# Reordering four stretches of a two-block fp32 transformer kernel: normalization boundaries, memory attention, the first output product, and the scan product

## The chip, the cores and the metric

The kernel runs on one NeuronCore of a Trainium2 chip, in one launch. The metric is the device time of one execution, in microseconds (us). Three runs of the kernel before are shown; their median is what a prediction is compared with. Engines are named as in the profile: PE is TensorE's matmuls, PEld its weight loads, DVE is VectorE, ACT is ScalarE, POOL is GpSimd, SP is SyncE, which here only issues DMAs.

## The reference, cut to what matters

One sequence of 512 positions with 1024 features passes through two blocks. All is fp32.

```
first block:   p = rms_norm(x) @ w_in ; pooling, stick-breaking attention, memory attention, each gated
               kv = rms_norm(mem) @ w_mem_kv     (mem has 256 positions; its q and k are normed per head)
               x = x + concat(pool, stick, memory) @ w_out
second block, for layer 0 and 1:
               m = mixer(rms_norm(x))            (0: retention + neighbourhood attention, 1: SSD scan)
               x = x + rms_norm(m)
               f = conv_geglu(rms_norm(x) @ w_up) @ w_down
               x = x + rms_norm(f)
scan mixer:    xbc = silu(conv5(h @ w_xbc)) ; dt = softplus(h @ w_dt + bias) ; z = h @ w_z ; scans ; @ w_out
rms_norm(v) = v * rsqrt(mean(v^2) + 1e-6) * gain
```

## The kernel before, in words

**Layout.** Activations lie features first: x is 8 tiles of 128 features by 512 positions. Every product runs over weight tiles of 128 output features, and a tile is 8 blocks of 128x128 (22 for the down products).

**Three matmuls for one.** Weights and activations are split into a rounded high part and the rest: ACT copies `w_hi` from the loaded `raw` slot (L309), DVE subtracts to get `w_lo` (L316), over `raw` itself. Each block product is three matmuls (L352 to L354): high by high, high weight by low activation, low weight by high activation. So a tile of 8 blocks is 24 matmuls of 512 columns.

**The ring.** Weights come through a ring of 5 slots. SP loads slot q once PE has finished slot q-5 (L301). `hi_to(act, q)` and `lo_to(dve, q)` emit the splits up to slot q at that point of ACT's or DVE's program; `split_ahead(name, t)` (L326) says how far ahead of tile t they run. Every engine works through its own list in order, and waits on semaphores counted by the others.

**A normed product.** The gain is folded into the activation split, and the norm's factor is applied to the product's rows afterwards. So a product can start before the sum of squares is known. `lead_pe` (L356) works on the first 4 tiles (2 for in1) at once, one block of the contraction at a time, as each low part `a_lo[k]` becomes ready. Later, at tile `SUMS[name][0]` (5 for all), `pre_sums_pe` (L429) sums the squares over partitions with a matmul by ones, into the bank of tile `SUMS[name][1]`; ACT takes Ln and Exp (`roots_act`, L437), and DVE refines the root (`roots_dve`, L443: one halving, three dependent operations). Only then can DVE take or scale the first product tile.

**A boundary** (three of them, `boundary_act` L503 and `boundary_dve` L513): after a mixer or FFN product, the root of its sum of squares comes first, then for each of the 8 tiles k DVE scales `m[k]` (L499), adds it to x (L501), and makes `a_lo[k-1]` (L417); ACT makes `a_hi[k]` (L413) and the square (L421) between. PE meanwhile repeats some matmuls whose result is not used (L486), then waits for the first `a_lo`. At the very end the last root is followed by eight pairs of scale and add, each followed by a store of 256 KB from SP (L2306 to L2308).

**Memory attention and out1** (`one_pe` from L1298, `one_act` from L1446, `one_dve` from L1600): PE interleaves the products of mem_kv, the scores (L1233), the turns of the probabilities (L1247) and the values (L1258) of four steps with the first output product's lead (`out1_half`, 4 tiles together). DVE has in one list the head norms (`half_norm`, `norm`: three dependent operations and one more, L456 to L458 and L1539), the low parts of the mixed activation (L1544), the maxima (`top`, L1550), the reciprocals (`invert`, L1559) and the copies of turned probabilities (`turned`, L1566); ACT has the exponentials (L1399) and the scaling of the probabilities by the reciprocals (`norms`, L1409).

**The first output product's tail** (L2351 to L2355 on ACT, L2398 to L2407 on DVE): for each tile t the lists hold: split slot t+4; add tile t to x; a_hi, square; a_lo and the sum of squares of the tile before. Slots 8 to 11 from the start of out1 are the first four of in2, whose lead comes next.

**The scan product xbc** (24 tiles, `xbc_act` L1804, `xbc_dve` L1832). Beside its lead runs the small product for dt (`dt_part`, 3 matmuls for each k). For each tile DVE scales the PSUM bank (L528), ACT writes the middle tap (L1817), DVE adds four taps (L1840), which frees the bank, and ACT applies silu (L1807). PE needs a free bank for tile 7 on: tile 7 takes the bank of tile 0. After tile 23 come two z tiles, and then `begin(0)` of the scans (L1875), which waits for the silu of all 24 tiles.

```
def split_ahead(name, t):   # name in SUMS, so for xbc too
    return PLAN[name]["slot0"] + max(min(t, 5) + 8, t + AHEAD)
...
for t in range(24):         # xbc_dve
    lo_to(dve, split_ahead("xbc", t))
    scale_dve(dve, "xbc", t, nrm_x[1])
    ...
    if t:
        taps(t - 1)
```

## Time and profile before

| | |
|---|---|
| median of 3 runs | 1825.57 us (1823.8 to 1826.84) |
| the profiled execution | 1822.33 us, of which its span is 1820.6 us |
| PE busy | 1752.2 us (96%), 8246 matmul instructions |
| DVE busy | 1164.6 us (64%) |
| ACT busy | 783.4 us (43%) |
| POOL busy | 177.5 us (10%) |
| memory traffic | 144.44 MB read, 2.10 MB written |
| chain that ended last | PE 80%, DVE 12%, ACT 5% |

PE is busy nearly all the time, so time can come only from the 68 us in which it is not (1820.6 - 1752.2) or in which its granted clock is low (a matmul at the lower clock counts as busy for longer). The idle time is read by stage, since each has another releaser.

### The profile page before, as it was taken

The page shows a single profiled execution, that of the slowest core. Times are in us where ns is not written, and L with a number is a line of the kernel's source. Part 1 is how long each engine was busy: PE and PEld are TensorE (multiplying, and loading weights), DVE is VectorE, ACT ScalarE, POOL GpSimd, SP SyncE. Part 2 cuts the span into 40 slices and gives each one's busy share as a digit, 9 for nine tenths or more (in the row PEclk, how much of TensorE's full clock was granted, in tenths as well). Part 3 has the DMA queues.
Part 4 walks back from the last instruction along what each step waited for, and adds up shares of the span by engine and source line. Part 5 has one row for each costly group of instructions (what it writes and reads, how often), then busy time and mean ns, then how long its engine had stood idle before and what let it go on. Part 6 is the DMA issues. An engine that isn't in the chain of part 4 may idle for free.

```text
span 1820.6 us, 20806 instructions
## 1 busy us (share of the span) xinstructions
PE 1752.2 (96%) x8246; PEld 1371.7 (75%) x8246; DVE 1164.6 (64%) x1577; ACT 783.4 (43%) x1326; POOL 177.5 (10%) x202
## 2 busy tenths in 40 slices
PE   9999898899999999999999999999899999999996
PEld 6777777676667888888877786777578788888884
DVE  4575754776758787663355998576674678766333
ACT  4465642452235454442232453655462445444220
POOL 0311000320000011110000000211220001111000
PEclk9999999999999999999999999999999999999998
DMA  5211223222112332333322222101112132323331
GB/s 215 93 58 47 70 82 108 87 63 66 56 46 73 117 103 93 96 98 101 96 67 87 81 93 69 35 29 43 35 35 93 58 116 94 103 93 93 100 99 55
DMA packets 42752, 147.88 MB, mean 81 GB/s; under 512 B 5152, under 2 KB 6304, under 8 KB 42528
## 3 DMA queue, kind: packets, MB, share of 16 engines
q1 hardware_dynamic: 39168, 138.43, 23.5%
q10 hardware_dynamic: 3488, 8.12, 1.3%
q8 instruction: 66, 1.08, 0.2%
q14 instruction: 30, 0.25, 0.0%
HBM read 144.44 MB, written 2.10 MB: 80 GB/s over the span
## 4 chain that ended last, share of the span: by engine, by line
PE 80%; DVE 12%; ACT 5%; issue 1%; DMA 1%; ACTq 0%; POOL 0%; DVEq 0%
PE bank L352 22%; PE bank L353 22%; PE bank L354 22%; DVE cv L1840 4%; DVE w_lo L316 2%; PE bank L1941 1%; ACT w_hi L309 1%; PE bank L1902 1%; PE bank L1914 1%; PE bank L698 1%; PE bank L711 1%; DVE bank L528 1%; PE bank L1923 1%; PE bank L1187 1%; PE bank L1186 1%
## 5 line engine op out<-in xcount | busy, mean ns | idle before, releaser
L352 PE MATMUL bank<-a_hi,w_hi 128*128 128x512 f32 x1504 | 606.6, 403 | 18.6 <-DVE cv L1840 6.7
L316 DVE TENSOR_TENSOR w_lo<-raw,w_hi 128x1024 fp32r<-128x1024 f32 (+1 forms) x264 | 335.1, 1273 | 413.6 <-ACT w_hi L309 412.8
L354 PE MATMUL bank<-a_hi,w_lo 128*128 128x512 f32 x1504 | 589.8, 392 | 0.0
L353 PE MATMUL bank<-a_lo,w_hi 128*128 128x512 f32 x1504 | 589.7, 392 | 0.0
L309 ACT ACTIVATE w_hi<-raw 128x1024 fp32r<-128x1024 f32 (+1 forms) x264 | 274.1, 1042 | 372.4 <-DMA raw<-in_w_down 142.6
L352 PEld LDWEIGHTS bank<-a_hi,w_hi 128*128 128x128 f32 x1504 | 284.9, 189 | 101.8 <-issue 28.0
L353 PEld LDWEIGHTS bank<-a_lo,w_hi 128*128 128x128 f32 x1504 | 284.9, 189 | 64.5 <-issue 7.2
L354 PEld LDWEIGHTS bank<-a_hi,w_lo 128*128 128x128 f32 x1504 | 284.6, 189 | 60.5
L1060 ACT ACTIVATE u<-bank,par 128x512 f32<-128x512 f32 x88 | 68.5, 779 | 176.2 <-DVE bank L528 176.2
L352 PE MATMUL bank<-g_hi,w_hi 128*128 128x512 f32 x352 | 137.0, 389 | 0.0
L353 PE MATMUL bank<-g_lo,w_hi 128*128 128x512 f32 x352 | 137.0, 389 | 0.0
L354 PE MATMUL bank<-g_hi,w_lo 128*128 128x512 f32 x352 | 137.0, 389 | 0.0
L1103 POOL TENSOR_TENSOR gv<-u 128x512 f32<-128x512 f32 x44 | 57.1, 1299 | 564.1 <-DVE u L1079 564.1
L2056 ACT ACTIVATE em<-bank,lbias 128x128 f32<-128x128 f32 x256 | 70.4, 386 | 23.4 <-PE bank L1924 23.1
L2196 DVE TENSOR_TENSOR em<-em,gmat 128x512 f32<-128x512 f32 x64 | 50.0, 787 | 41.6 <-ACT em L2056 41.3
L354 PEld LDWEIGHTS bank<-g_hi,w_lo 128*128 128x128 f32 x352 | 66.1, 188 | 13.8
L353 PEld LDWEIGHTS bank<-g_lo,w_hi 128*128 128x128 f32 x352 | 66.1, 188 | 13.6
L352 PEld LDWEIGHTS bank<-g_hi,w_hi 128*128 128x128 f32 x352 | 66.1, 188 | 13.6
L1840 DVE SCALAR_TENSOR_TENSOR cv<-bank,par,cv 128x510 f32<-128x510 f32 (+1 forms) x96 | 71.7, 748 | 2.5
L1079 DVE SCALAR_TENSOR_TENSOR u<-bank,par,u 128x511 f32<-128x511 f32 x88 | 66.0, 750 | 3.1
L1076 DVE SCALAR_TENSOR_TENSOR u<-bank,par,u 128x511 f32<-128x511 f32 x88 | 65.1, 740 | 0.0
L528 DVE TENSOR_TENSOR bank<-bank,nrm_u 128x512 f32<-128x512 f32 x88 | 60.9, 692 | 0.7 <-PE bank L354 0.7
(362 smaller groups left out, 2096.1 us busy)
## 6 DMA issues: line engine op xcount, KB each, us to landing
raw<-in_w_up SPq DMA_DIRECT2D x88, 512.0 KB, 3.7
raw<-in_w_in SPq DMA_DIRECT2D x52, 512.0 KB, 3.7
raw<-in_w_out SPq DMA_DIRECT2D x32, 512.0 KB, 3.7
raw<-in_w_down SPq DMA_DIRECT2D x32, 512.0 KB, 3.5
raw<-in_w_xbc SPq DMA_DIRECT2D x24, 512.0 KB, 3.7
raw<-in_w_z SPq DMA_DIRECT2D x16, 512.0 KB, 3.6
raw<-in_w_down SPq DMA_DIRECT2D x16, 384.0 KB, 3.1
x<-in_xT ACTq DMA_DIRECT2D x4, 512.0 KB, 7.1
```

The source lines that it names most:

```text
L309: nc.scalar.activation(w_hi[:, q % RING, 0:w], raw[:, q % RING, 0:w], ACT.Copy).then_inc(hi_done, 1)
L316: nc.vector.tensor_tensor(w_lo[:, q % RING, 0:w], raw[:, q % RING, 0:w], w_hi[:, q % RING, 0:w].bitcast(F32), ALU.subtract).then_inc(lo_do ...
L352: nc.tensor.matmul(out, wh, rhs_hi[:, k, :], start=k == first, stop=False)
L353: nc.tensor.matmul(out, wh, rhs_lo[:, k, :], start=False, stop=False)
L354: return nc.tensor.matmul(out, wl, rhs_hi[:, k, :], start=False, stop=stop)
L528: nc.vector.tensor_tensor(tile_bank(name, t)[:, :], tile_bank(name, t)[:, :], r, ALU.mult).then_inc(scaled, 1)
L1060: nc.scalar.activation(u[:, t % 4, :], tile_bank(name, t)[:, :], ACT.Identity, scale=pcol(f"ffn_w{layer}", 3 * t + 1), bias=pcol(f"ffn_b{l ...
L1076: nc.vector.scalar_tensor_tensor(out=ut[:, 1:S], in0=pt_[:, 0:S - 1], scalar=pcol(w, 3 * t), in1=ut[:, 1:S], op0=ALU.mult, op1=ALU.add).th ...
L1079: nc.vector.scalar_tensor_tensor(out=ut[:, 0:S - 1], in0=pt_[:, 1:S], scalar=pcol(w, 3 * t + 2), in1=ut[:, 0:S - 1], op0=ALU.mult, op1=ALU ...
L1103: nc.gpsimd.tensor_tensor(gv[:, i % 2, :], u[:, 2 * i % 4, :], u[:, 2 * i % 4 + 1, :], ALU.mult).then_inc(prod, 1)
L1840: nc.vector.scalar_tensor_tensor(out=dst, in0=tile_bank("xbc", tile)[:, a + by:b + by], scalar=pcol("conv_w", 5 * tile + tap), in1=dst, op ...
L2056: e = nc.scalar.activation(em[:, n % 4, c * P:(c + 1) * P], bank[4 + n % 2][:, c * P:(c + 1) * P], ACT.Exp, bias=lbias[:, c, d, h:h + 1])
```

## The change

Four edits, joined:

1. **Boundaries and closing.** In the three boundaries the low part of tile k-1 stands between the scaling and the addition of tile k, where it stood behind both. At the end DVE scales all eight tiles but adds only three of them; for tiles 0 to 4 PE adds x and the scaled product in PSUM with ten matmuls by the identity (the five by x are issued before the root is known), ACT copies the banks to x, and SP stores those first.
2. **Memory attention's order.** On ACT and DVE the roots and norms of the keys' halves, the reciprocals, the maxima and the turned copies stand in another order, with low parts later; the split of out1's slot 4 stands inside the attention.
3. **First output product's tail.** The one loop is written out: four additions first, then splits and low parts in groups, slots up to 11 at fixed places.
4. **Scan product.** The sum of squares is taken at the last step of the lead (k=7, after the dt matmuls) where it stood before tile 5; ACT's and DVE's splits of slots 5 and 6 stand behind the roots. `split_ahead` for xbc is 5 slots ahead of tiles 0 to 6 (it was 8), then 11, then t+4. DVE scales a tile ahead of the split. The dt transposes stand before tile 5 (6 before).

No matmul, load or element operation is dropped but the five additions of the closing.

```diff
 LEAD = {"in1": 2, "out1": 4, "in2": 4, "out2": 4, "up0": 4, "xbc": 4, "up1": 4}
-SUMS = {"in1": (5, 7), "in2": (5, 7), "up0": (5, 7), "xbc": (5, 6), "up1": (5, 7)}
+SUMS = {"in1": (5, 7), "in2": (5, 7), "up0": (5, 7), "xbc": (4, 6), "up1": (5, 7)}
 DT_BANK, CUM_BANK, TOTAL_BANK, CST_BANK = 0, 3, 4, 5
...
             return PLAN[name]["slot0"] + (8 + t // 2 if t < 8 else t + AHEAD)
+        if name == "xbc":
+            return PLAN[name]["slot0"] + max(min(t, 6) + 5, t + AHEAD)
         return PLAN[name]["slot0"] + max(min(t, 5) + 8, t + AHEAD) if name in SUMS else last_slot(name, t) + AHEAD
...
         for t in range(LEAD[name], PLAN[name]["tiles"]):
-            if t == before:
+            if t == before and name != "xbc":
                 pre_sums_pe(pe, name, home, event, pre, squares, S)
...
-    def update_dve(dve, v, k, m, r):
+    def scaled_dve(v, k, m, r):
         nc.vector.tensor_tensor(m[:, k, :], m[:, k, :], r, ALU.mult).then_inc(m_done, 1)
+
+    def added_dve(dve, v, k, m):
         dve.wait_ge(m_done, KT * v + k + 1)
         nc.vector.tensor_tensor(x[:, k, :], x[:, k, :], m[:, k, :], ALU.add).then_inc(x_done, 1)
+
+    CLOSED = 5
+    closing, closed = sem("closing"), sem("closed")
+
+    def closing_pe(pe):
+        tile_gone(pe, "down1", 5)
+        for k in range(CLOSED):
+            nc.tensor.matmul(bank[(5, 6, 7, 0, 1)[k]][:, :], C["ident"], x[:, k, :], start=True, stop=False)
+        for k in range(CLOSED):
+            pe.wait_ge(m_done, 3 * KT + k + 1)
+            nc.tensor.matmul(bank[(5, 6, 7, 0, 1)[k]][:, :], C["ident"], m_ffn[:, k, :], start=False, stop=True).then_inc(closing, 1)
+
+    def closing_act(act):
+        for k in range(CLOSED):
+            act.wait_ge(closing, k + 1)
+            nc.scalar.activation(x[:, k, :], bank[(5, 6, 7, 0, 1)[k]][:, :], ACT.Copy).then_inc(closed, 1)
...
             square_act(x, k, squares)
-        hi_to(act, PLAN[next_name]["slot0"] + 6)
+        hi_to(act, PLAN[next_name]["slot0"] + (4 if next_name == "xbc" else 6))
         roots_act(act, next_event, tile_bank(next_name, SUMS[next_name][1])[:, :], nrm_next[0], nrm_next[1])
...
         for k in range(KT):
-            update_dve(dve, v, k, m, nrm[1])
+            scaled_dve(v, k, m, nrm[1])
             if k:
                 low_dve(dve, pre, x, k - 1, gain, a_hi, a_lo)
+            added_dve(dve, v, k, m)
         low_dve(dve, pre, x, KT - 1, gain, a_hi, a_lo)
...
             add_dve(dve, pre, k, squares)
-        lo_to(dve, PLAN[next_name]["slot0"] + 6)
+        if next_name != "xbc":
+            lo_to(dve, PLAN[next_name]["slot0"] + 6)
         roots_dve(dve, next_event, tile_bank(next_name, SUMS[next_name][1])[:, :], *nrm_next)
...
         square(2)
+        roots(2)
+        square(3)
         hi_to(act, split_ahead("mem_kv", 2))
-        square(3)
+        roots(3)
         hi_to(act, split_ahead("mem_kv", 3))
-        roots(2)
-        roots(3)
         high(0)
...
         exps(2)
+        hi_to(act, split_ahead("out1", 0))
         norms(2)
...
-        def kv_tile(t):
-            if t < 2:
-                lo_to(dve, split_ahead("mem_kv", t))
+        def take_kv(t):
             tile_ready(dve, "mem_kv", t)
             nc.vector.tensor_tensor(kv[:, t, :], tile_bank("mem_kv", t)[:, 0:MEM], nrm_mem[:, 1, :], ALU.mult).then_inc(evac, 1)
+
+        def kv_tile(t):
             lo_to(dve, split_ahead("mem_kv", t))
+            take_kv(t)
...
                 kv_tile(1)
-                kv_tile(2)
-                kv_tile(3)
+                take_kv(2)
+                half_norm(2)
+                norm(2)
+                take_kv(3)
+                lo_to(dve, split_ahead("mem_kv", 2))
+                half_norm(3)
+                lo_to(dve, split_ahead("mem_kv", 3))
             if p == 0:
...
             if p == PAIRS - 1:
-                half_norm(2)
-                half_norm(3)
-                norm(2)
                 low(0)
...
         norm(1)
+        invert(0)
+        low(2)
+        top(1)
+        turned(0, 0)
         norm(3)
-        low(2)
+        invert(1)
+        turned(0, 1)
         low(3)
+        top(2)
         low(4)
-        invert(0)
-        top(1)
+        turned(1, 0)
         low(5)
-        turned(0, 0)
-        turned(0, 1)
-        invert(1)
-        top(2)
-        turned(1, 0)
         turned(1, 1)
...
         top(3)
+        lo_to(dve, split_ahead("out1", 0))
         mem_gate(0)
...
         mem_gate(1)
+        low(7)
+
+    def out1_act(act):
+        first = PLAN["out1"]["slot0"]
+
+        def normed(t):
+            tile_gone(act, "out1", t)
+            high_act(x, t, "mix_pre0", a_hi)
+            square_act(x, t, sq_2)
+
+        hi_to(act, first + 4)
+        normed(0)
+        normed(1)
+        hi_to(act, first + 5)
+        normed(2)
+        normed(3)
+        hi_to(act, first + 7)
+        normed(4)
+        hi_to(act, first + 8)
+        normed(5)
+        hi_to(act, first + 10)
+        normed(6)
+        hi_to(act, first + 11)
+        normed(7)
+
+    def out1_dve(dve):
+        first = PLAN["out1"]["slot0"]
+
+        def added(t):
+            tile_ready(dve, "out1", t)
+            nc.vector.tensor_tensor(x[:, t, :], x[:, t, :], tile_bank("out1", t)[:, :], ALU.add).then_inc(evac, 1)
+
+        def low(t):
+            low_dve(dve, PRE_IN2, x, t, "mix_pre0", a_hi, a_lo)
+            if t:
+                add_dve(dve, PRE_IN2, t, sq_2)
+
+        lo_to(dve, first + 4)
+        for t in range(4):
+            added(t)
+        low(0)
+        low(1)
+        lo_to(dve, first + 5)
+        low(2)
+        low(3)
+        lo_to(dve, first + 7)
+        added(4)
+        low(4)
+        lo_to(dve, first + 8)
+        added(5)
+        low(5)
+        lo_to(dve, first + 10)
+        added(6)
+        low(6)
+        lo_to(dve, first + 11)
+        added(7)
         low(7)
...
+    def beside_lead_pe(pe, k):
+        dt_part(pe, k)
+        if k == KT - 1:
+            pre_sums_pe(pe, "xbc", SUMS["xbc"][1], EV_XBC, PRE_XBC, sq_x, S)
+
     def dt_turn(pe):
...
         pe = nc.tensor
-        if t == 6:
+        if t == 5:
             dt_turn(pe)
...
         for t in range(24):
+            scale_dve(dve, "xbc", t, nrm_x[1])
             lo_to(dve, split_ahead("xbc", t))
-            scale_dve(dve, "xbc", t, nrm_x[1])
             if t == 1:
...
         for k in range(KT):
-            sp_.wait_ge(x_done, 3 * KT + k + 1)
+            if k < CLOSED:
+                sp_.wait_ge(closed, k + 1)
+            else:
+                sp_.wait_ge(x_done, 3 * KT + k - CLOSED + 1)
             sp_.dma_start(dr["out"][:, k, :], x[:, k, :]).then_inc(out_done, 16)
...
-        for t in range(KT):
-            hi_to(act, split_ahead("out1", t))
-            tile_gone(act, "out1", t)
-            high_act(x, t, "mix_pre0", a_hi)
-            square_act(x, t, sq_2)
+        out1_act(act)
         hi_to(act, PLAN["in2"]["slot0"] + 6)
...
         act.dma_start(tri[:, :, :], dr["tri"]).then_inc(tri_load, 16)
-        hi_to(act, PLAN["xbc"]["slot0"] + 7)
+        hi_to(act, PLAN["xbc"]["slot0"] + 5)
         xbc_act(act)
...
         roots_act(act, EV_POST3, bank[4][:, :], nrm_b[:, 0, :], nrm_b[:, 1, :])
+        closing_act(act)
...
-        for t in range(KT):
-            lo_to(dve, split_ahead("out1", t))
-            tile_ready(dve, "out1", t)
-            nc.vector.tensor_tensor(x[:, t, :], x[:, t, :], tile_bank("out1", t)[:, :], ALU.add).then_inc(evac, 1)
-            if t:
-                low_dve(dve, PRE_IN2, x, t - 1, "mix_pre0", a_hi, a_lo)
-            if t > 1:
-                add_dve(dve, PRE_IN2, t - 1, sq_2)
-        low_dve(dve, PRE_IN2, x, KT - 1, "mix_pre0", a_hi, a_lo)
-        add_dve(dve, PRE_IN2, KT - 1, sq_2)
+        out1_dve(dve)
         lo_to(dve, PLAN["in2"]["slot0"] + 6)
...
         boundary_dve(dve, 1, EV_POST1, rows(nrm_b), m_ffn, PRE_XBC, "mix_pre1", sq_x, "xbc", EV_XBC, nrm_x)
-        lo_to(dve, PLAN["xbc"]["slot0"] + 7)
         xbc_dve(dve)
...
         roots_dve(dve, EV_POST3, bank[4][:, :], *rows(nrm_b))
-        for k in range(KT):
-            update_dve(dve, 3, k, m_ffn, nrm_b[:, 1, :])
+        for k in range(CLOSED):
+            scaled_dve(3, k, m_ffn, nrm_b[:, 1, :])
+        for k in range(CLOSED, KT):
+            scaled_dve(3, k, m_ffn, nrm_b[:, 1, :])
+            if k > CLOSED:
+                added_dve(dve, 3, k - 1, m_ffn)
+        added_dve(dve, 3, KT - 1, m_ffn)
...
         spin_between(pe, "xbc")
-        normed_pe(pe, "xbc", EV_XBC, sq_x, beside_xbc_pe, lambda k: dt_part(pe, k))
+        normed_pe(pe, "xbc", EV_XBC, sq_x, beside_xbc_pe, lambda k: beside_lead_pe(pe, k))
         ssd_pe(pe)
...
         post_sums_pe(pe, 3, EV_POST3, sq_b, nrm_b[:, 0, :])
+        closing_pe(pe)
```

## Rows read from the trace of the kernel before

**Rows 1.** Who waited for whom, PE, whole span (us in total, times, longest us)
```profile
PE bank L352 <- DVE cv L1840: 6.7, 2, 3.8
PE bank L352 <- DVE a_lo L417: 6.1, 3, 2.2
...
PE bank L352 <- DVE w_lo L316: 4.7, 2, 3.1
...
PE bank L1247 <- ACT prob L1409: 3.1, 2, 2.7
...
PE bank L1716 <- DVE a_lo L417: 2.0, 1, 2.0
...
PE bank L1233 <- DVE mk L1539: 1.5, 1, 1.5
```

**Rows 2.** DVE in order of time, first boundary (start, duration, idle before)
```profile
572.28 0.69 DVE L501 TENSOR_TENSOR x<-x,m_mix 128x512 f32<-128x512 f32 x1
572.89 0.68 DVE L499 TENSOR_TENSOR m_mix<-m_mix,nrm_m 128x512 f32<-128x512 f32 x1
...
574.22 0.75 DVE L417 SCALAR_TENSOR_TENSOR a_lo<-x,par,a_hi 128x512 fp32r<-128x512 f32 x1
```

**Rows 3.** ACT in order of time, second boundary
```profile
942.64 0.72 ACT L413 ACTIVATE a_hi<-x,par 128x512 fp32r<-128x512 f32 x1 [3.74 <-DVE x L501]
```

**Rows 4.** Busy time in the second boundary (columns: engines, PEclk, DMA, GB/s)
```profile
946.00:948.00 2.00, 2.00 (x6) 1.60 (x5) 1.97 (x4) 1.25 (x3) 0.00 (x0) 0.50 0.00 0
```

**Rows 5.** DVE in order of time, memory attention
```profile
219.03 0.42 DVE L456 TENSOR_TENSOR msq<-mhalf,mrs 128x256 f32<-128x256 f32 x1
...
222.61 0.22 DVE L1559 RECIPROCAL mstat<-mstat 128x2 f32<-128x2 f32 x2
```

**Rows 6.** DVE in order of time, out1's tail
```profile
276.59 1.23 DVE L316 TENSOR_TENSOR w_lo<-raw,w_hi 128x1024 fp32r<-128x1024 f32 x1 [1.00 <-ACT w_hi L309]
...
280.67 1.23 DVE L316 TENSOR_TENSOR w_lo<-raw,w_hi 128x1024 fp32r<-128x1024 f32 x1 [0.99 <-ACT w_hi L309]
```

**Rows 7.** Chain that ended last, in2's lead (start, length, what)
```profile
282.81 0.43 PE bank L353
...
287.31 0.23 PE bank L352
```

**Rows 8.** Weight loads, issue to landing (KB each, median us)
```profile
raw<-in_w_out SPq DMA_DIRECT2D x32, 512.0 KB, 3.7
```

**Rows 9.** PE in order of time: the scan product's sum and the scans' begin
```profile
979.19 1.02 PE L432 MATMUL bank<-sq_x,cst 128*128 128x512 f32 x2
...
1109.45 0.66 PE L1875 MATMUL bank<-cst,xbc 128*128 128x128 f32 x4 [1.53 <-ACT xbc L1807]
```

**Rows 10.** DVE in order of time, scan product
```profile
983.88 1.23 DVE L316 TENSOR_TENSOR w_lo<-raw,w_hi 128x1024 fp32r<-128x1024 f32 x1
...
1096.15 1.21 DVE L316 TENSOR_TENSOR w_lo<-raw,w_hi 128x1024 fp32r<-128x1024 f32 x1
...
1100.89 1.22 DVE L316 TENSOR_TENSOR w_lo<-raw,w_hi 128x1024 fp32r<-128x1024 f32 x1
...
1108.65 0.68 DVE L2184 TENSOR_TENSOR zt<-bank,nrm_x 128x512 f32<-128x512 f32 x1
```

**Rows 11.** Groups by line and form, scan product (x count | busy us, mean ns | idle before)
```profile
L316 DVE TENSOR_TENSOR w_lo<-raw,w_hi 128x1024 fp32r<-128x1024 f32 x21 | 25.6, 1218 | 4.8 <-ACT w_hi L309 4.8
```

**Rows 12.** Chain that ended last, the closing
```profile
1801.96 0.86 PE bank L494 x2
...
1807.44 0.70 DVE m_ffn L499
...
1817.47 0.69 DVE x L501
```

**Rows 13.** The stores (KB each, median us to landing)
```profile
out<-x SPq DMA_DIRECT2D x8, 256.0 KB, 2.0
```

**Rows 14.** Busy time by stretch, the start of the kernel (last column GB/s)
```profile
6.00:8.00 2.00, 2.00 (x5) 0.88 (x4) 0.00 (x0) 0.05 (x1) 0.00 (x0) 1.00 1.03 418
```

## The prediction

> **What bounds the kernel now.** Read the busy times first: TensorE works in 1752 of 1820.6 us, so the matmuls are the floor, and this change drops none of them. What it can win is TensorE's idle time and the stretches at the lower clock. The next view is who waited for whom on TensorE [rows 1]; it names the stages: 6.7 us for the four taps of the scan product (two waits), 4.7 us for low parts of weights (two waits, both in the lead of in2), 3.1 us for scaled probabilities and 1.5 us for a normed key (both in memory attention), and at each boundary some 2 us for the first low part (three of the 6.1 and 2.0; the 2.2 is the kernel's start, which the change leaves). Each is a chain through VectorE's list, whose order the change alters. The last thing is the tail after TensorE's last matmul. A tile of 8 blocks is 24 matmuls at 0.227 us from start to start, 5.45 us; I use that throughout.
>
> **Boundaries.** Addition to scaling takes 0.61 us from start to start, scaling to the dependent addition 0.72, so the first low part starts 1.94 us after the first addition [rows 2]. In the new order it stands behind the second scaling and could start at 1.22, but it needs ACT's high part: the addition's 0.69 us and ACT's 0.72 [rows 3] with two hand-overs of some 0.04 make 1.50. So the lead starts 0.44 us sooner, three times. For later tiles the pace becomes 2.16 us (1.50 and 0.66) where it was 1.99, against 2.73 us that TensorE needs for one step of the lead: hidden; eight tiles cost VectorE 1.3 us there, and the sums that follow it are not needed before the lead's end. Bounds for each boundary: 0 (ACT later than worked out) and 0.72. In the second boundary the matmuls after the wait ran at the clock of 1.2 GHz [rows 4], for about 3.2 us, a loss of 1.5 us; after the same wait of 2.0 us in the other two they did not. I count no gain from that, and keep plus or minus 1.5 us in the range. The Trainium skill ("TensorE: Matmul & The Clock Gate", Part 1) says that the number of slow matmuls of one kernel varies from run to run; by it such a loss may come or go unchanged, and no gain could be booked.
>
> **Memory attention.** The 1.5 us wait [rows 1] ends with the key's norm, which stood behind the splits of two more slots. It now stands after the third kv tile, about 5 us sooner, while TensorE still works on the values: gone. The 2.7 us wait ends with the scaled probabilities, which need the reciprocals. Between 219.03 and 222.61 VectorE did the second key's norm and three low parts ahead of them [rows 5]: 3.6 us, now behind. The maxima before them start 1.3 us sooner. So the probabilities come 4.9 us sooner, and 4.2 (2.7, and 1.5 since TensorE arrives sooner) are needed: gone, by 0.7. Next late are the first turned copy and the fourth low part, each within 0.3 us of TensorE; I give them 0.2. The short waits further on stay. ACT's split of slot 4 inside (1.05 us) lies in its wait for the third pair of reciprocals; VectorE's (1.23) in its wait for the values. **4.1 us**; bounds 1.5 and 4.3.
>
> **First output product.** The tail is a ping-pong: split high, split low, addition, high part, square, and again, 4.08 us from one low split to the next [rows 6], eight times, so in2's third and fourth slots came late (1.5 and 3.1 us). After the 3.1 us TensorE ran at the lower clock: a matmul each 0.43 us, not 0.23, from 282.81 to about 287.3 [rows 7], a loss of 4.5 x (1 - 0.23/0.43) = 2.1 us. In the new order the low split of in2's fourth slot waits only for its load, which starts when tile 6 is done, 5.45 us before the product ends: load 3.7 [rows 8], high 1.05, low 1.23, hand-overs 0.4: ready 0.9 us after the end. The lead needs it for its fourth tile, 9 matmuls or 2.0 us in. Slot 2 starts a tile sooner. The additions behind a split only feed low parts that are needed one each 2.73 us. **6.8 us** (4.7 and 2.1), with 1.1 us to spare; bounds 3 (slot late by 2 us, the clock falls once more) and 6.8.
>
> **Scan product.** The sum started at 979.19 [rows 9], the root was ready 4.7 us later at 983.88 [rows 10]. The last step of the lead began its large matmuls 5.45 + 2.73 before the sum, at 971.0; there the sum now stands, and 0.44 sooner by the boundary: 970.6, root at 975.25. ACT must be free; so the splits of slots 5 and 6, whose ring places the lead holds, stand behind. The squares' last addition ends some 3 us ahead. From the root on VectorE has been the bound: 124.8 us to 1108.65, almost without a gap, 4.74 us a tile [rows 10] against TensorE's 5.45. Now two splits more (2 x 1.14 = 2.3), and waits for high parts of 2.6 where they were 4.8 [rows 11] (0.8 for slot 5's load, 0.9 behind dt's logarithm, 0.9 at the table load): ready at 975.25 + 124.8 + 2.3 - 2.2 = 1100.15, the scans' begin 0.8 later at 1100.95 where it was 1109.45 [rows 9]. TensorE's own list, without the 6.7 us of waits, would be through its z tiles at 1107.9 - 6.7 - 0.44 = 1100.8, or 2 less without the slow clock after the 3.8 us wait; against that some 1.3 us for tile 12, whose low split is now made only in VectorE's ninth turn. Both ends meet. **8.4 us**, its boundary's 0.44 included; bounds 4 (waits at each of tiles 8 to 14) and 10.
>
> **Closing.** Before: 16 operations from 1807.44, the last beginning at 1817.47 [rows 12]. Now 11, and independent, so 0.61 each: the last begins at 1813.54, 3.9 us sooner. Beside it TensorE does ten fp32 products of 0.86 us [rows 12]: five by x from 1803.8 to 1808.1, then five, 1812.4; ACT copies each in at most 0.72, the last by 1813.2. The dependent end is a store, 2.0 us to landing [rows 13]: issued at 1814.25, landed 1816.25. Eight stores of 256 KB at the 418 GB/s of [rows 14] take 0.63 each; from the first issue at 1809.75 they land at the earliest at 1809.75 + 2.0 + 7 x 0.63 = 1816.2: no loss, but no slack. SP's list is in order, so tile 5's store waits 0.8 us for the fifth copy; this is in the sum. **3.9 us**; bounds 0.9 (the last five products at half clock: copies end at 1817.3) and 3.9. By the Trainium skill's limit for one core ("DMA: Bandwidth & Descriptors", Where 436 GB/s comes from: about 358 GB/s where HBM binds) the stores would end 0.7 us later and the sum would be 23.4; the trace's 418 GB/s, a load, is above it.
>
> **Sum.** 0.9 (two boundaries) + 4.1 + 6.8 + 8.4 + 3.9 = 24.1 us. The profiled execution, 1822.33, would become 1798.2. It lies 3.2 us under the median of the runs, 1825.57, which becomes **1801.5**.
>
> **Rivals.**
> - *Some waits form again.* For: the attention's and the tail's slots have 0.7 and 1.1 us to spare, dt's steps put ACT and VectorE in lockstep for four tiles. Then attention keeps 1.5, out1 3, scan 6, closing 3: 0.9 + 13.5 = 14.4 us, 1811.2. Half of such a loss gives 1806. Against: each wait was followed with durations of this trace. Chance 0.25.
> - *More than the sum.* The second boundary keeps its clock too (1.5) and the scans begin on TensorE's own time (1.6): 27.2 us, 1798.4. Chance 0.12.
> - *Slower: VectorE waits for a high part in every tile of the scan product.* Splits now run 5 slots ahead, not 8, and behind the scaling. The three waits before took 1.6 us each (4.8 in [rows 11]). If twenty tiles each wait so, VectorE needs 6.35 us a tile, over TensorE's 5.45: 32 us on the critical path, 1833.5. It decides from 24.1/20 = 1.2 us a tile. Against: ACT's middle tap, silu and split (0.78, 0.62, 1.05) fit in the 4.1 us of low split and taps before the next, as in the steady half of the stage, where VectorE waits for none. Chance 0.02.
> - *It doesn't carry through*: later stages wait for something that does not move with TensorE (loads of tables, GpSimd). Then nothing is left, 1825. All such loads are issued by lists that move along. Chance 0.02.
>
> The forecast itself has 0.59. A measurement of this kernel tells 0.2% (3.7 us) from no change. **Range** 1797.5 to 1809: from the second rival to two thirds into the first. Faster 0.96, within 0.2% 0.02, slower 0.02.
>
> **What would show it.** Right: TensorE's waits for taps and for low parts of weights gone or under 1.5 us together; no wait over 1 us at the turns; the scan's sum before its lead ends and the scans' begin 17 to 21 us sooner on the clock of the span (4.1 + 6.8 + 0.4 + 8.4 = 19.7); three waits of 1.5 us at the boundaries; the last VectorE operation 11 after the root. Wrong: waits for low parts of weights in tiles 8 to 20 of the scan product, a lower clock in the closing, or stores that land over 2.5 us after the last addition.

## The result, and the profile after

The changed kernel runs in **1795.6 us** (median of 4 runs, 1794.5 to 1796.4), the kernel before beside it in 1826.1; the ratio is 0.9837 [0.9822, 0.9853]. It is faster, as forecast, but by more than the range allowed: 1795.6 lies 1.9 us below its low end and 5.9 under the forecast of 1801.5. Profiled: 1822.33 before, 1794.47 after (span 1792.7), 27.9 us less where the sum said 24.1. Granted clock over the span: 0.987 before, 0.996 after. Two runs, one of before (clock 0.81) and one of the out1 part alone (0.75), were 11% and 21% longer than the others and are left out of all medians below.

The clock of the span counts stretches in which TensorE has no work, so it overstates the difference. The closing, kernel before and kernel after (stretch, length, then busy time and count of PE, PEld, DVE, ACT, POOL; PEclk, DMA share, GB/s):

```profile
1806.00:1820.00 14.00, 0.00 (x0) 0.00 (x0) 11.82 (x18) 0.00 (x0) 0.00 (x0) 0.50 0.40 150
1782.00:1792.00 10.00, 5.48 (x13) 1.90 (x11) 6.96 (x12) 2.98 (x5) 0.00 (x0) 1.00 0.57 210
```

Fourteen microseconds at half clock are 0.004 of before's 0.013, and they slow no matmul.

Who waited for whom on TensorE, kernel after (us in total, times, longest us):

```profile
PE bank L2011 <- ACT em L2144: 6.0, 4, 4.6
PE bank L354 <- DVE a_lo L419: 5.1, 3, 2.1
...
PE bank L1799 <- DVE a_lo L419: 1.5, 1, 1.5
...
PE bank L354 <- DVE w_lo L316: 1.2, 1, 1.2
...
PE bank L1280 <- DVE pt L1590: 0.8, 1, 0.8
...
PE bank L1269 <- ACT prob L1431: 0.4, 1, 0.4
```

Against [rows 1]: the 6.7 us for taps and the 1.5 for the key are gone, low parts of weights fell from 4.7 to 1.2, the probabilities from 3.1 to 0.4, and each boundary waits 1.5 where it was 2.0. The forecast named these marks, and they hold. One of its marks does not: the scans' begin came 23.6 us sooner (1109.45 in [rows 9], 1085.89 after), where it said 17 to 21. Of its marks of error one shows, stores that land late behind the last addition (below).

The scan product, kernel after, TensorE, VectorE and TensorE in order of time (start, duration, what):

```profile
956.11 1.02 PE L434 MATMUL bank<-sq_x,cst 128*128 128x512 f32 x2
...
960.80 0.68 DVE L1931 TENSOR_TENSOR dt_ch<-bank,nrm_x 64x512 f32<-64x512 f32 x1
...
1085.09 0.68 DVE L2272 TENSOR_TENSOR zt<-bank,nrm_x 128x512 f32<-128x512 f32 x1
```

From root (4.7 us after the sum) to VectorE's last turn are 124.3 us; it was 124.8 in [rows 10], and the forecast said 124.9.

Busy time by stretch, kernel after (columns as above):

```profile
946.00:948.00 2.00, 2.00 (x10) 1.63 (x9) 1.28 (x2) 0.97 (x2) 0.00 (x0) 1.00 0.00 0
1294.00:1296.00 2.00, 1.40 (x3) 0.68 (x4) 1.01 (x2) 2.00 (x7) 0.00 (x0) 0.58 0.00 0
1786.00:1788.00 2.00, 1.60 (x4) 0.38 (x2) 2.00 (x4) 1.48 (x3) 0.00 (x0) 1.00 0.87 321
1788.00:1790.00 2.00, 0.00 (x0) 0.00 (x0) 1.00 (x2) 0.23 (x1) 0.00 (x0) 1.00 0.85 312
1790.00:1792.00 2.00, 0.00 (x0) 0.00 (x0) 0.00 (x0) 0.00 (x0) 0.00 (x0) 1.00 0.95 356
```

PEclk 0.50 is TensorE's clock of 1.2 GHz, 1.00 that of 2.4. Where the second boundary of before stood at 0.50 [rows 4], no stretch of after's boundaries does; the low clock is left at the start, behind two waits in the steps of in2 and behind the 4.6 us wait late in the SSD stage (second row). The last three rows are the closing: TensorE is through by 1788 and VectorE by 1789, while the DMA engines are nearly full to the end.

The closing, kernel after, in order of time:

```profile
1782.29 4.30 DVE L501 TENSOR_TENSOR m_ffn<-m_ffn,nrm_b 128x512 f32<-128x512 f32 x7
...
1784.82 5.25 SPq L2399 DMA_DIRECT2D out<-x  x8
...
1787.63 0.60 ACT L521 ACTIVATE x<-bank 128x512 f32<-128x512 f32 x1 [0.26 <-PE bank L516]
1787.72 1.28 DVE L505 TENSOR_TENSOR x<-x,m_ffn 128x512 f32<-128x512 f32 x2
```

VectorE's last addition ends at 1789.00, 6.7 us after the first scaling, just as forecast; the span ends 3.7 us behind it, where before it was 1820.6 - 1818.16 = 2.4.

**Where the time went.** The same matmul's start in both traces gives the shift at any place; its steps, stretch by stretch, beside the forecast's terms:

| stretch | forecast | traces |
|---|---|---|
| memory attention | 4.1 | 4.7 |
| out1's tail and in2's lead | 6.8 | 7.5 |
| in2's steps (shorter slow stretch) | 0 | 0.4 |
| first and third boundary | 0.9 | 0.9 |
| second boundary and scan product | 8.4 | 0.45 + 1.5 (slow clock) + 8.7 = 10.6 |
| late SSD stage (shorter slow stretch) | 0 | 1.2 |
| closing | 3.9 | 2.75 |
| sum | 24.1 | 28.0 |

The other 2.1 us of the miss of 5.9 are between the profiled execution and the runs: before's lay 3.8 under the median of the four runs beside after and 3.2 under that of three, which the forecast carried over; after's lay only 1.2 under.

### The profile page after: what moved, and what is told of

Same layout as the page of the kernel before. It is cut to its first block, busy times and chain, and to the rows that moved or that the text cites. A ratio compares the mean times of both kernels' runs of the same rounds, so it can differ in the third digit from the quotient of the medians.

```text
span 1792.7 us, 20845 instructions
## 1 busy us (share of the span) xinstructions
PE 1752.7 (98%) x8266; PEld 1369.8 (76%) x8266; DVE 1160.3 (65%) x1572; ACT 785.8 (44%) x1331; POOL 177.6 (10%) x202
## 4 chain that ended last, share of the span: by engine, by line
PE 81%; DVE 11%; ACT 4%; issue 1%; DMA 1%; ACTq 1%; POOL 0%; DVEq 0%
PE bank L354 23%; PE bank L356 22%; PE bank L355 22%; DVE cv L1928 4%; DVE w_lo L316 2%; PE bank L2029 1%; PE bank L1990 1%; PE bank L2002 1%; PE bank L720 1%; PE bank L733 1%; DVE bank L550 1%; ACT w_hi L309 1%; PE bank L2011 1%; PE bank L1209 1%; ACT em L2144 1%
```

## The experiments

Two theories. **A**: the surplus is stretches at the lower clock behind waits of TensorE, which vanish with the waits. **B**: the parts are worth more together than the sum of each. For the closing: the stores' throughput, or SP's ordered list. Runs sent together share a chip and the runs of before, whose median was 1822.5 to 1826.1 from chip to chip, so parts are compared by the ratio to before (its 95% interval in brackets). A thousandth is 1.8 us. "Filler" means fp32 matmuls by constants into a bank that is started anew afterwards; they change no result. The edits are shortened: `constants` stands for `cst[:, 0:4, :]` as one row, and semaphore increments are left out.

| run | median us | ratio to before | granted clock |
|---|---|---|---|
| scan part alone | 1815.09 | 0.9944 [0.9932, 0.9956] | 0.987 to 0.990 |
| out1 part alone | 1814.22 | 0.9950 [0.9933, 0.9968] | 0.984 to 0.991 |
| attention part alone | 1816.77 | 0.9957 [0.9944, 0.9970] | 0.986 to 0.989 |
| closing alone | 1820.88 | 0.9981 [0.9972, 0.9990] | 0.987 to 0.990 |
| boundary order alone | 1821.56 | 0.9982 [0.9971, 0.9992] | 0.985 to 0.988 |
| before, three waits filled | 1819.23 | 0.9972 [0.9962, 0.9981] | 0.987 to 0.992 |
| before, all but the scan product filled | 1812.77 | 0.9940 [0.9927, 0.9953] | 0.994 |
| after again | 1796.10 | 0.9849 [0.9835, 0.9863] | 0.993 to 0.994 |
| after without the attention part | 1797.72; 1803.22 | 0.9860 [0.9845, 0.9876]; 0.9889 [0.9873, 0.9904] | 0.995 to 0.998; 0.991 to 0.994 |
| after, two store queues | 1795.07 | 0.9843 [0.9830, 0.9857] | 0.993 to 0.995 |
| after, last four stores only | 1796.83 | 0.9855 [0.9840, 0.9870] | 0.992 to 0.994 |
| after, four waits filled | 1792.90 | 0.9828 [0.9815, 0.9842] | 0.997 to 0.999 |
| after, more filled | 1791.59 | 0.9824 [0.9811, 0.9838] | 0.997 to 0.999 |
| after, filled, stores spread | 1789.95; 1791.04 | 0.9817 [0.9803, 0.9830]; 0.9819 [0.9805, 0.9833] | 0.998 to 1.000; 0.998 to 0.999 |

### Each part alone

The five parts of the diff, each applied to before by itself. Scan product: `SUMS["xbc"]`, `split_ahead`, the sums in the lead, the turns at 5, splits behind the scaling. Expected:

> Before with the scan product's part alone (the sums in its lead, the roots two tiles earlier, splits behind the scaling). Theory A (each part is worth what its own stretch of the two traces shows; what the forecast missed are stretches of TensorE at the lower clock behind waits that went): 10.2 us less than before, 2.2 of them the eleven half-speed matmuls behind the 3.8 us wait, and perhaps 1 more from a shorter slow stretch late in the SSD stage. Theory B (the forecast's terms are right for each part and the surplus comes from the parts together): 8.0 us less.

10.2 us less by the ratio (8.0 to 12.4): A's figure, with B's 8.0 at the edge of the interval. In its trace the stretch from the second boundary to the scans' begin is 9.3 us shorter. But it is no clean 9.3 under before elsewhere: the run has slow matmuls at 92 and at 225 us, the latter behind the 2.7 us wait of memory attention, where the profiled run of before has the same wait and none. Busy time of the same two stretches in this run and in the next (columns as above):

```profile
14.00:16.00 2.00, 2.00 (x6) 1.56 (x5) 2.00 (x4) 2.00 (x4) 0.23 (x1) 0.50 0.99 406
225.00:227.00 2.00, 2.00 (x7) 1.75 (x8) 1.66 (x4) 2.00 (x9) 0.00 (x0) 0.50 0.00 0
```

The first output product: `out1_act` and `out1_dve` in place of the two loops. Expected:

> Before with the first output product's new order alone. Theory A: 7.5 us less (two waits of 1.5 and 3.1, their restarts, 2.2 to 2.5 of lower clock). Theory B: 6.8 or less, since the split of the product's first slot has kept its old place in memory attention.

```profile
14.00:16.00 2.00, 2.00 (x11) 1.61 (x10) 2.00 (x4) 2.00 (x4) 0.32 (x1) 1.00 1.00 406
225.00:227.00 2.00, 2.00 (x14) 1.17 (x12) 0.45 (x3) 1.58 (x4) 0.00 (x0) 1.00 0.00 0
```

9.1 us less by the ratio (interval 5.8 to 12.2), 7.5 of them in its own stretch. Between 14 and 16 us nothing of the kernel differs between these two programs, yet one ran 6 matmuls and the other 11. So the low clock behind a given wait comes and goes. The Trainium skill ("TensorE: Matmul & The Clock Gate", Part 1) says that the number of slow matmuls of one kernel varies from run to run; these rows, of two programs that are alike up to there, agree.

Memory attention: the orders in `one_act` and `one_dve` alone.

> Before with memory attention's order alone. Theory A: 4.7 us less. Theory B: 4.1 us less, or less than that where the old tail of the output product, in which VectorE sets the pace, gives TensorE's gain back.

7.8 us less by the ratio (5.5 to 10.2), more than either theory said (4.7 and 4.1): a miss of both, whose cause is open; in its trace the stretch itself gave 4.7. The closing alone:

> Before with the closing additions alone. The forecast's term is 3.9 us, the two traces show 2.75. Both theories: 2.7 to 2.9 us less than before; 3.9 would mean that the closing is disturbed only in the joined kernel.

3.5 us less by the ratio (1.8 to 5.1), which holds the expected 2.7 to 2.9 and also 3.9; its trace decides: 10.46 us from the first scaling to the span's end, 10.45 in after, 13.16 in before. And the order in `boundary_dve` alone (`scaled_dve`, low part, `added_dve`):

> Before with the boundaries' order alone (scaling, low part, addition). The forecast booked 0.44 at each of three boundaries, 1.3 us. Theory A (clock): the wait after the second boundary falls from 2.0 to 1.5 us and the seven half-speed matmuls behind it go: 2.8 us less. Theory B: they stay or come and go whatever the wait: 1.3 us less. The profile shows it at 945 to 949 us.

2.2 us less by the medians, 3.3 by the ratio (1.5 to 5.3). The seven slow matmuls at 946 us are gone in its trace, as A says, but seven others stand at 997 us, in the scan product, where VectorE sets the pace, and more at 92 and 225 us. The interval holds both A's 2.8 and B's 1.3, so the time decides nothing. What decides for this boundary is the count over all profiles: behind its 2.0 us wait the clock was low in all five that have it (before and the first four parts), behind 1.5 us or less in none of the thirteen others. At the first boundary the same 2.0 us wait brought it in none of six profiles, at the third in one of six. The ratios of the five add up to 1.86% (34 us), the joined change has 1.63%, and 1.51% when run again: so the parts don't need one another, as B would have it. If anything each alone is worth more, with intervals that leave this open.

### The lower clock, taken away in before

The cleanest test of A takes no wait away and fills them.

```diff
     def lead_pe(...):
                     bank_clear(pe, name, t)
+                    if name == "in2" and t > 1:
+                        spin_pe(pe, constants, tile_bank(name, t), 2 * t - 3)
                     pe.wait_ge(lo_done, last_slot(name, t) + 1)
     def spin_between(pe, name):
-        spin_pe(..., 6)
+        spin_pe(..., 8 if name == "xbc" else 6)
     def ssd_pe(pe):   # after part_z, last group
+            else:
+                spin_pe(pe, constants, bank[7], 4)
```

> Before, no wait removed, but filler matmuls (fp32 by constants, into a bank about to be started anew) put into waits of TensorE: one ahead of the third tile of in2's lead and three ahead of the fourth, two more at the second boundary, four in the 4.6 us wait late in the SSD stage. Theory A (the surplus is the lower clock behind waits): the slow stretches at 282, 946 and 1317 us go, 4.4 us less than before in the median. Theory B (the surplus has another cause, or the clock falls whatever is in the wait): 0, or some tenths more for fillers that overrun.

5.1 us less by the ratio (3.5 to 6.9), 4.5 by the medians; A said 4.4, B 0. The stretches at 282 and 946 us are gone, and that at 1317 us is half as long: four fillers leave 1.2 us of its wait. Others came, at 326 us, at 988 us in the scan product and at 1436 us behind the third boundary. Then the same in every wait but the scan product's, with two more at the first and third boundary too; in the memory scores and turns the wait for the operand was moved behind the filler. Beside the lines above:

```diff
-        spin_pe(pe, spin, tile_bank("in1", 1), 8)
+        spin_pe(pe, spin, tile_bank("in1", 1), 10)
+            spin_pe(pe, constants, tile_bank("in1", STICK_FROM), 3)   # stick_scores, p == 0
+            spin_pe(pe, constants, bank[0], 1)                         # mem_scores, s == 0
+            spin_pe(pe, constants, bank[2], 3)                         # mem_turn, first unit
+        spin_pe(pe, constants, tile_bank("in2", 8), 2)                 # before na_windows(pe, 0)
+                spin_pe(pe, constants, tile_bank("in2", 9), 3)         # step s == 1
```

> Before with fillers in every wait of TensorE outside the scan product behind which a slow stretch was seen in some run: start 2, first stick scores 3, memory scores 1, first turned probabilities 3, in2's lead 1 and 3, the steps of in2 2 and 3, each boundary 2, SSD 4. Theory A (the surplus over the forecast's sum is lower clock, in the profiled run and more in the timed ones): 8 to 10 us less than before, and the filled version of after beside it (whose closing is 0.5 us shorter still) is only 22 to 25 us faster than this, near the forecast's sum without its 2.1 us of slow clock. Theory B (the parts are worth more together): less than 4 us under before, the filled after over 29 us faster.

In2's lead in this run, TensorE in order of time:

```profile
276.05 0.50 PE L352 MATMUL bank<-a_hi,w_hi 128*128 128x512 f32 x1 [0.67 <-DVE w_lo L316]
...
276.85 2.74 PE L488 MATMUL bank<-cst 128*128 128x512 f32 x6
280.12 0.50 PE L352 MATMUL bank<-a_hi,w_hi 128*128 128x512 f32 x1 [0.54 <-DVE w_lo L316]
280.46 0.39 PE L353 MATMUL bank<-a_lo,w_hi 128*128 128x512 f32 x1
280.69 0.39 PE L354 MATMUL bank<-a_hi,w_lo 128*128 128x512 f32 x1
```

The low part comes as late as ever (3.5 us from the product's last matmul to its next); but with three fillers (L488, each two records) in the wait the matmuls behind it start 0.23 us apart, not 0.43 as in [rows 7]. The kernel is **10.5 us faster than before (1823.3 on this chip) without one low part, key or probability coming by another order**; the ratio's interval is 8.6 to 13.3 us. Its five runs lie within 0.6 us where those of before spread over 4.5. A expected 8 to 10, B under 4. Three slow stretches are left in its trace. Two are in the scan product, where VectorE sets the pace: TensorE's lead over before is 8.6 us ahead of that stage and 8.6 behind it. The third is late in the SSD stage, behind waits of 1.2 and 0.8 us that four fillers leave:

```profile
1311.00:1313.00 2.00, 2.00 (x8) 1.81 (x9) 1.03 (x2) 1.97 (x6) 0.00 (x0) 0.50 0.00 0
```

Between this version and the filled after (next section) are 21.7 us, A's 22 to 25 nearly, B's 29 not at all. By stretch between these two traces: start 0.5, attention 4.1, out1 5.1, the boundaries 1.4, scan 8.9, closing 3.2 with the spread stores; less 1.4 for a slow stretch at 330 us that is in the later trace.

### The lower clock, taken away in after

```diff
-        spin_pe(pe, spin, tile_bank("in1", 1), 8)
+        spin_pe(pe, spin, tile_bank("in1", 1), 10)
     def two_pe(pe):
+        bank_clear(pe, "in2", 8)
+        spin_pe(pe, constants, tile_bank("in2", 8), 2)
         tile_gone(pe, "in2", 7)
         na_windows(pe, 0)
...
+            if s == 1:
+                bank_clear(pe, "in2", 9)
+                spin_pe(pe, constants, tile_bank("in2", 9), 2)
     # and four in ssd_pe, as above
```

> After, with fillers in four waits behind which its trace shows slow matmuls: ten instead of eight fp32 matmuls at the start (1.7 of a 2.1 us wait), two at 315 us, two at 329 us, four in the wait late in the SSD stage. Theory A: 1.4 + 3 x 0.8 = 3.8 us less than after. Theory B: 0 or more.

2.7 us less than after by the medians (on another chip), 2.1 in the profiled runs: a miss by 1.1 to 1.7. The stretches behind all four waits are gone. The one late in the SSD stage, for which 0.8 was expected, had cost nothing: TensorE's lead over after is 2.2 us ahead of it and 2.2 behind. By 18 us TensorE is 1.6 us ahead, and it loses this again at 89 us. TensorE in order of time, this run:

```profile
89.37 3.86 PE L1198 MATMUL bank<-p 64*128 64x256 f32 x16 [3.43 <-ACT vt L1389]
```

and the same sixteen matmuls behind the same wait in after:

```profile
91.02 2.43 PE L1193 MATMUL bank<-p 64*128 64x256 f32 x16 [3.51 <-ACT vt L1384]
```

A wait that cost only itself in after now brings the low clock too. The fillers at the start did not move it there: a second profile of after itself, no line changed, has both, slow matmuls from 13.7 us on and these:

```profile
90.95 3.48 PE L1193 MATMUL bank<-p 64*128 64x256 f32 x16 [3.42 <-ACT vt L1384]
```

Which of the waits brings the low clock is not the program's alone to say. So three fillers go there, and one more at each boundary:

```diff
     def stick_scores(pe, p):
+        if p == 0:
+            bank_clear(pe, "in1", STICK_FROM)
+            spin_pe(pe, constants, tile_bank("in1", STICK_FROM), 3)
         pe.wait_ge(vtc, p + 1)
     def spin_between(pe, name):
-        spin_pe(..., 6)
+        spin_pe(..., 7)
```

> The filled version of after with three more fillers in the 3.4 us wait ahead of the first stick scores (there the low clock had moved: sixteen matmuls took 3.86 us, 2.43 in after) and one more at each of the three boundaries. Theory A: 1.4 us less than the filled version, near 1790.9 at best, and its granted clock stays at 0.998 or above in every run. Theory B: no change.

1.3 us less than the version before it (medians; the ratios, 0.9824 and 0.9828, can't tell them apart). The sixteen take 2.43 us again. Two slow stretches were left in its profiled run, at 331 us behind the 1.9 us that two fillers leave of a wait, and at 1293 us behind the 1.2 and 0.8 us that four leave; the clock was 0.997 in one run where 0.998 was the least expected. Over the six profiles with fillers, no slow stretch stands behind a wait that they fill to within 0.7 us; behind those two waits one stands in two of four and in three of six.

### Attention's part in the joined kernel

After with the old orders of memory attention:

> After with memory attention's old order, so that the other three parts stand alone. If the parts add up (each worth what its stretch shows): 4.7 us more than after, 1800.3. If attention alone was worth what its own timing said (8.5 us under before) in the joined kernel too: 1804. If its part has no worth beside the others: 1795.6 to 1797.

By the ratio 2.3 thousandths, 4.2 us, more than after, near the 4.7 of adding parts; the medians gave 2.1, but on different chips. So both were run on one:

> The changed kernel itself, as the measure for the three beside it on one chip: 30 us under before, granted clock 0.994 to 0.996.

> After with memory attention's old order, beside after on one chip. Its own stretch: 4.7 us more than after; with the lower clock that its waits can bring in some runs, up to 6. Under 3 would say that the later stages give a part of it back.

After itself lay 27.2 us under before here (1796.10 and 1823.3), not 30, at a clock of 0.993 to 0.994. Without the attention part: 1803.22 against 1796.10, 7.1 us more, over the 6 expected; the two profiled runs differ by 4.0 (1800.25, 1796.21). The three timed runs above it have 0.991 to 0.993 as their clock, after's 0.993 to 0.994. The old order costs its 4.1 to 4.7 us of waits, and on this chip lower clock besides; on the other chip the same program ran in 1797.72 at 0.995 to 0.998, 5.5 us less. So what the part is worth in the joined kernel is open between 4 and 7 us. Slow matmuls behind the old order's 2.7 us wait at 225 us stand in three profiles, those of the scan part alone, of the boundary order alone and of the first run without attention (PEclk 0.50).

### The closing

Two queues: the stores of tiles 4 and 5 issued by ACT.

```diff
     def closing_act(act):
+        act.wait_ge(closed, CLOSED)
+        act.dma_start(dr["out"][:, 4, :], x[:, 4, :])
+        act.wait_ge(x_done, 3 * KT + 1)
+        act.dma_start(dr["out"][:, 5, :], x[:, 5, :])
     # SP: for k in (0, 1, 2, 3, 6, 7)
```

> After, with the stores of tiles 4 and 5 issued by ACT behind its copies, so that SP's list has six stores and tile 7's does not stand behind tile 6's start-up by the same cause. If the queue's order is what lengthened the closing: the last store issues at once behind the last addition, 0.5 to 0.6 us less than after. If the stores' throughput binds: 0 to 0.2.

From the first scaling (1782.40) to the span's end (1792.89) are 10.49 us; in after 10.45. The list is not the cause. Four stores:

```diff
-            sp_.dma_start(dr["out"][:, k, :], x[:, k, :])
+            if k > 3:
+                sp_.dma_start(dr["out"][:, k, :], x[:, k, :])
```

> After without the stores of tiles 0 to 3: tiles 4 to 7 are stored as before and in the same order, the first half of the output is not written. If the stores' throughput lengthened the closing: the last store lands some 2.0 us after its issue and the span ends about 2.5 us after the last addition where after has 3.7, 0.9 to 1.2 less. If it is the fixed time of a store or of the queue: no change.

Four-store run, the closing in order of time:

```profile
1788.32 0.60 ACT L521 ACTIVATE x<-bank 128x512 f32<-128x512 f32 x1 [0.26 <-PE bank L516]
1788.41 1.28 DVE L505 TENSOR_TENSOR x<-x,m_ffn 128x512 f32<-128x512 f32 x2
1789.01 1.81 SPq L2400 DMA_DIRECT2D out<-x  x4
```

and its busy time:

```profile
1790.00:1792.00 2.00, 0.00 (x0) 0.00 (x0) 0.00 (x0) 0.00 (x0) 0.00 (x0) 0.78 1.02 382
```

No change: the span ends at 1793.5, 3.8 us after the last addition. My reading of throughput, all eight stores in one stream, is refuted, and the rows suggest another. The fifth tile's copy frees SP's list at 1789.0, and from there four stores of 262 KB at 382 GB/s (0.69 us each) are left: 4.5 us to the span's end, with the first four stores or without (after: from 1788.26 to 1792.74). The first five issue 0.86 us apart, as the products come, and mostly drain between. So what counts is how many stores stand behind the fifth copy. If so, tile 5's store should go out earlier:

```diff
-        for k in range(CLOSED): scaled_dve(3, k, ...)
-        ...
+        for k in (0, 1, 2, 5, 3): scaled_dve(3, k, ...)
+        closing_add(5)
+        for k in (4, 6, 7): scaled_dve(3, k, ...)
+        closing_add(6)
+        closing_add(7)
     # SP: for k in (0, 1, 5, 2, 3, 4, 6, 7)
```

> The same, and in the closing tile 5 is scaled and added by VectorE ahead of tiles 3 and 4, so that its store issues third and the last three stores don't bunch. If the stores' throughput binds: 0.2 to 0.3 us less from the first scaling to the span's end than in the version beside it. If the last store's own time binds: 0.

Its busy time in the closing:

```profile
1783.00:1785.00 2.00, 0.88 (x2) 0.05 (x1) 2.00 (x4) 1.08 (x2) 0.00 (x0) 1.00 1.02 381
1785.00:1787.00 2.00, 0.00 (x0) 0.00 (x0) 0.11 (x1) 0.00 (x0) 0.00 (x0) 1.00 1.02 381
```

First scaling 1778.40, end 1788.35: 9.95 us, against 10.46 in the version beside it, 0.51 less and more than the 0.2 to 0.3 expected. It is what the count of stores gives: three are left behind the fifth copy instead of four, 0.69 less, and that copy ends 0.18 later after the first scaling (6.12 us, 5.94 in after). The same on after's chip:

> The filled version of after with its stores spread, on the same chip as after: if the gain is real and not the chip's, 4 to 6 us less than after, with a granted clock of 0.998 to 1.0 in every run.

1791.04 against 1796.10, **5.1 us less than after on the same chip**, and 1.8% less than before: it beats both kernels. Its profiled run still has one slow stretch (330 us, 1.2 us).

## Why the prediction was right, and where it was not

**Boundaries, attention, out1: right in mechanism and size.** Three times 0.42 to 0.45 (0.44 forecast). Attention 4.1 between the two filled versions (4.1 forecast). The 0.6 more in the plain traces is not clock, as neither has a slow stretch between 18 and 280 us: from the first matmul of the stick-breaking values to the first memory scores are 3.4 us in the filled before and 3.9 in before, so the key came 0.5 sooner there. Out1 5.1 without clock (4.7 forecast) and 7.5 with it (6.8). No wait formed again; the first rival did not come, nor did VectorE wait in every tile: low parts of weights cost TensorE 1.2 us, the 1.3 of the forecast.

**"I count no gain from that, and keep plus or minus 1.5 us in the range" is the step that failed.** The forecast took low clock as an event of one place: 2.1 us booked in out1, 1.5 left out, none looked for elsewhere. It is a cost that the waits of TensorE from 2.0 to 4.6 us carry here with some chance; behind the 1.5 us that are left at the boundaries of after no profile showed it. The trace of one execution shows only that execution's draw. That before had the same wait at two other boundaries at full clock was no reason to book nothing: the second boundary's slow stretch stood in all five profiles with its 2.0 us wait and in none with 1.5. One profile could not show that, but the 1.5 us belonged in the sum with a chance, not at nothing. On one chip the account is: before to filled before 10.5 us, filled before to filled after 21.7 (21.2 without the spread stores), after lies 5.1 above filled after (4.5 without them). Total 27.2 = 21.2 of waits and 6.0 (10.5 less 4.5) of clock. The forecast had 22.0 and 2.1. The split rests on differences of medians whose ratios have intervals of about 2.4 us either way, and both filled versions keep some slow stretches, so it is an estimate. The first comparison gave 30.5 us (1826.1 less 1795.6), 3.3 more than this chip; the two ratios' intervals overlap, and what makes the difference is open.

**"It lies 3.2 us under the median of the runs", carried over, failed for the same reason.** The 3.2 was most likely low clock that the timed runs had and the profiled one had not: before's runs go from 1820.6 at a clock of 0.988 to 1826.8 at 0.984 on one chip. A kernel with fewer waits has less of it, and after's offset is 1.2. With 3.8 us missing in the sum these 2.1 make the 5.9.

**Closing: 3.9 forecast, 2.75 measured.** "From the first issue at 1809.75 they land at the earliest at 1809.75 + 2.0 + 7 x 0.63" counted an unbroken stream from the first store on. But stores two to five issue every 0.86 us and leave gaps, and the last four queue behind the fifth copy: by the forecast's own times 1813.25 + 4.45 = 1817.7 where it had 1816.7 for the span's end (last addition's end and 2.45), 1.0 of the 1.15 us. The rate was also off: 381 GB/s in full stretches, not the 418 of a load. The Trainium skill's 358 GB/s ("DMA: Bandwidth & Descriptors", Where 436 GB/s comes from) is under what the stores reached here.

**Scan product: 8.0 forecast without its boundary, 8.7 to 8.9 measured.** The root came 8.2 us sooner without the clock, as worked out (8.2); VectorE's stage shrank by 0.5 where 0.1 more was forecast, though it waited 3.2 us for high parts and not 2.6. So its other work took 1.2 us less than I allowed. Most of it is a wait that I had left inside the 124.8, for the logarithm of dt; before's row of it is

```profile
L1781 DVE TENSOR_TENSOR dtt<-dtt,dtv 128x256 f32<-128x256 f32 x1 | 0.4, 427 | 0.9 <-ACT lndt L1799 0.9
```

and in after VectorE has no wait there.

**Range.** Its low end was about the second rival's, which had 1.5 us for clock beside the 2.1 in out1, 3.6 together. Clock was worth about 6.0, so the end should have stood some 2.4 us lower, at 1795.1; the measured 1795.6 would have been only just inside.

## What to carry to other kernels

A wait of TensorE is to be priced at its length plus the half-speed matmuls that may follow, and the second part as a chance over runs, not as what the one profiled execution shows; the spread of the runs and of their granted clocks hints at how much of it a kernel holds, once stretches without matmuls are set aside. Where TensorE is not what sets the pace, as in the scan product here, the slow matmuls cost nothing. Where a wait can't be removed, matmuls into a free bank that filled it to within 0.7 us kept the clock in every profile here and cost nothing that could be seen: 10.5 us of 1823 in before, about as much as the scan product's whole restructuring. At the end of a kernel count the stores that are still to issue behind the last computed tile, at the rate of full stretches (0.69 us each here).

## What the runs showed that was not expected

- The low clock does not follow the program alone. The start of one kernel's matmuls ran at 0.50 and another's, with identical work so far, at 1.00, both behind the wait of 2 to 3 us for the first low part. Two profiles of after, the same program, differ too: the sixteen matmuls at 91 us took 2.43 us in one and 3.48 in the other.
- Filling the waits of before narrowed its spread: five runs lie within 0.6 us (1812.66 to 1813.28), runs of before on that chip between 1821.1 and 1825.5. Filling those of after did not: four runs within 2.0 us (1789.5 to 1791.5), after's own within 1.6.
- Medians of the unchanged kernel lie 3.6 us apart on different chips (1822.5 to 1826.1), about as much as a part of this change is worth, those of after 0.5 and those of after without its attention part 5.5. With runs of one kernel spread over 4 to 7 us on one chip, how much of this is the chip is open.
- Two DMA queues for the last stores gave nothing over one: 375 GB/s in the last full stretch of 2 us with two; with one, 356 in after and 375 and 382 in two versions of it.
